# Order of the down and gate/up pieces, source of the sigmoid, and order of the bias products in a mixture-of-experts loop

## What is computed

```python
def expert_block(args):
    xb, e = args
    gu = xb @ w_gu[e] + b_gu[e]
    gate = jnp.minimum(gu[:, :D_FF], SWIGLU_LIMIT)              # limit 7.0
    up = jnp.clip(gu[:, D_FF:], -SWIGLU_LIMIT, SWIGLU_LIMIT)
    hid = (up + 1.0) * gate * jax.nn.sigmoid(SWIGLU_ALPHA * gate)
    return hid @ w_dn[e] + b_dn[e]
```

## Time and profile before

| | us |
|---|---|
| median of 3 runs | 1810.24 |
| lowest and highest | 1800.36, 1814.44 |
| profiled execution | 1814.36 |
| its span, first to last instruction | 1812.5 |

### The profile page before, as it was taken

One profiled execution on the slowest core, in us unless ns is written; L12 is line 12 of the kernel. 1 busy time (PEld: TensorE's weight loads), 2 busy tenths in 40 slices (PEclk: granted clock), 3 DMA queues, 4 the chain that ended last, 5 costly groups with the idle time before them and its releaser, 6 DMA issues.

```text
span 1812.5 us, 20603 instructions
## 1 busy us (share of the span) xinstructions
PE 1600.7 (88%) x7124; PEld 737.2 (41%) x7125; DVE 362.9 (20%) x853; ACT 372.4 (21%) x723; POOL 121.8 (7%) x219
## 2 busy tenths in 40 slices
PE   6899999999999997978779998787999886998991
PEld 4565665666666653322223332222333222332330
DVE  3443442223231123110101110101011101011114
ACT  3443342354430020111101111111111111111111
POOL 0100000000000000100001110000011000010110
PEclk9889989899999997988989999889999998999995
DMA  7112112221208524899998999999899999579894
GB/s 254 63 47 73 47 47 93 71 70 47 93 1 300 196 102 176 351 406 417 414 406 312 403 364 412 408 414 408 337 404 352 407 411 399 243 308 411 330 382 156
DMA packets 108009, 477.36 MB, mean 263 GB/s; under 512 B 12899, under 2 KB 16848, under 8 KB 74530
## 3 DMA queue, kind: packets, MB, share of 16 engines
q1 hardware_dynamic: 99928, 461.77, 64.9%
q0 software_dynamic: 7808, 15.00, 2.5%
q10 hardware_dynamic: 234, 0.08, 0.0%
HBM read 471.26 MB, written 15.50 MB: 269 GB/s over the span
## 4 chain that ended last, share of the span: by engine, by line
PE 70%; DMA 17%; DVE 6%; issue 3%; SPq 2%; ACT 1%; DVEq 0%; ACTq 0%; POOL 0%; POOLq 0%
PE bank L578 30%; PE bank L961 20%; DMA ring<-in_w_gate_up 16%; PE bank L984 15%; PE bank L582 3%; PE bank L967 1%; DVE r_c L1322 1%; DVE r_kv L1319 1%; DVE r_v L1322 1%; DMA b_router_b<-in_b_router 1%; SPq L537 0%; SPq L544 0%; SPq L453 0%; DVE r_qk L1316 0%; DVE ring L1316 0%
## 5 line engine op out<-in xcount | busy, mean ns | idle before, releaser
L961 PE MATMUL bank<-ring,r_kv 128*64 128x512 f32 x2184 | 521.1, 625 | 98.2 <-DMA ring<-in_w_gate_up 98.2
L961 PEld LDWEIGHTS bank<-ring,r_kv 128*64 128x64 f32 x2184 | 157.3, 142 | 411.6 <-issue 309.4
L984 PE MATMUL bank<-ring,r_kv 128*64 128x512 f32 x1248 | 291.4, 610 | 0.7 <-ACT r_kv L1049 0.7
L578 PE MATMUL bank<-r_xt,ring 128*128 128x336 f32 x848 | 259.7, 462 | 2.0 <-DVE r_xt L1319 1.7
L1316 DVE TENSOR_SCALAR r_kv<-bank 128x512 f32<-128x512 f32 (+1 forms) x80 | 55.0, 687 | 928.2 <-PE bank L967 921.7
L578 PEld LDWEIGHTS bank<-r_xt,ring 128*128 128x128 f32 x848 | 163.5, 196 | 85.0 <-issue 15.9
L984 PEld LDWEIGHTS bank<-ring,r_kv 128*64 128x64 f32 x1248 | 93.1, 144 | 197.6 <-issue 196.6
L1049 ACT ACTIVATE r_xt<-bank 128x512 f32<-128x512 f32 x39 | 23.3, 598 | 520.8 <-PE bank L984 520.8
L578 PE MATMUL bank<-ring 128*128 128x336 f32 (+4 forms) x336 | 94.9, 423 | 4.1 <-DVE ring L1475 3.9
L1275 ACT ACTIVATE r_o<-r_kv 128x512 f32<-128x512 f32 x39 | 24.6, 632 | 324.0 <-DVE r_kv L1316 324.0
L582 PEld LDWEIGHTS bank<-const,r_v 64*128 64x128 f32 (+3 forms) x524 | 45.5, 139 | 79.3 <-DVE r_v L1322 44.5
(11 more groups left out here) (231 smaller groups left out, 992.1 us busy)
## 6 DMA issues: line engine op xcount, KB each, us to landing
ring<-in_w_gate_up SPq DMA_DIRECT2D x256, 1024.0 KB, 18.1
ring<-in_w_down SPq DMA_DIRECT2D x128, 1024.0 KB, 15.1
ring<-in_w_in SPq DMA_DIRECT2D x12, 2048.0 KB, 7.9
ring<-in_w_proj_b SPq DMA_DIRECT2D x2, 2048.0 KB, 8.4
ring<-in_w_proj_a SPq DMA_DIRECT2D x2, 2048.0 KB, 8.5
ring<-in_w_out SPq DMA_DIRECT2D x2, 2048.0 KB, 7.9
ring<-y_rows SPq DMA_DIRECT2D x4, 1024.0 KB, 7.9
ring<-in_w_uq SPq DMA_DIRECT2D x2, 1152.0 KB, 8.9
```

The costliest lines, as they stand in the source:

```text
L578: ins = pe.matmul(out, l, r, start=(n == 0), stop=(n == len(pairs) - 1), **kw)
L961: ins = pe.matmul(half(gate_bank if q < 2 else up_bank, q % 2), xg[:, k, :], w[:, 512 * q:512 * q + 512], start=False, stop=False, skip_gr ...
L984: ins = pe.matmul(half(out_bank, t), hidT[:, j, BLK * h:BLK * h + BLK], w[:, h, 512 * t:512 * t + 512], start=(j == 0 and h == 0), stop=(j ...
```

## The change

In PE's loop `gate_up(0)` moves behind `down(1)`, and the biases are split: those of the up bank stay ahead of the transposes of `hid`, those of the gate bank come behind them. So the gate bank stays readable until `hid` is made. ACT takes the sigmoid straight from the gate bank. As the gate is no longer limited ahead of it, the limit is put on the sigmoid's result (sigmoid grows with its argument, so its minimum with sigmoid(1.702 * 7) is the same) and, for the gate itself, into the last step. DVE's steps become: `up` as the clamp of up + 1 (1 is added once to the biases of the up half, ahead of the loop), `glu` as min(sigmoid, limit) times `up`, and `hid` as min(gate bank, 7) times `glu`. The step that wrote `gt` is gone; `pick` waits for the first k-tile of its block instead.

```diff
--- before.py
+++ after.py
@@ -37,6 +37,7 @@
 SCALE = float(np.float32((NOPE + ROPE) ** -0.5))
 EPS = 1e-6
 LIMIT, ALPHA = 7.0, 1.702
+SIG_LIMIT = float(1.0 / (1.0 + np.exp(-LIMIT * ALPHA)))
 NEG = -1e30
 
 
@@ -324,7 +325,7 @@
 
         xg = r3(r_kv[:, 0:512], 8)
         hidT = r3(r_kv[:, 512:1024], 4)
-        gt = r_kv[:, 1024:1536]
+        glu = r_kv[:, 1024:1536]
         up = r_kv[:, 2048:2560]
         sg = r_o[:, 0:512]
         gateT = r_o[0:NE, 2048:2048 + NT]
@@ -376,11 +377,11 @@
              "sig_ready", "qk_ready", "tail_done", "pad_set", "ones_set", "n_set", "lg_d", "lg_a", "gates_x", "gates4",
              "wprev_ready", "e_ready", "q_scaled", "hs_v", "hs_s", "hn_ready", "q_ready", "pmax", "pnorm", "mix_a",
              "x1_ss", "x1_v", "x1_s", "x2_ready", "chosen_set", "gate_x", "gate_e", "moe_tab", "stored", "stored_c"))
-        m_glu, gates_set, kr_in = sem("m_glu"), sem("gates_set"), sem("kr_in")
+        bgu_set, gates_set, kr_in = sem("bgu_set"), sem("gates_set"), sem("kr_in")
         w_if_set = sem("w_if_set")
-        (m_xrow, m_gath, m_xg, m_gt, m_sig, m_hid, m_yrow, m_gate, m_up, m_down, m_store, m_dve, m_pick, m_turn, m_hidT,
+        (m_xrow, m_gath, m_xg, m_sig, m_hid, m_yrow, m_gate, m_up, m_down, m_store, m_dve, m_pick, m_turn, m_hidT,
          fin_v, fin_ss, fin_s, fin_out, all_out) = map(sem, (
-             "m_xrow", "m_gath", "m_xg", "m_gt", "m_sig", "m_hid", "m_yrow", "m_gate", "m_up", "m_down", "m_store",
+             "m_xrow", "m_gath", "m_xg", "m_sig", "m_hid", "m_yrow", "m_gate", "m_up", "m_down", "m_store",
              "m_dve", "m_pick", "m_turn", "m_hidT", "fin_v", "fin_ss", "fin_s", "fin_out", "all_out"))
         m_rows_in, m_read = sem("m_rows_in"), sem("m_read")
         x_sent, yrow_free = sem("x_sent"), sem("yrow_free")
@@ -944,10 +945,10 @@
             def half(bank, t):
                 return bank[BLK * t:BLK * t + BLK, :]
 
-            def bias(b):
+            def bias(b, quarters):
 
                 pe.wait_ge(m_pick, b + 1)
-                for q in range(4):
+                for q in quarters:
                     pe.matmul(half(gate_bank if q < 2 else up_bank, q % 2), pick[32 * q:32 * q + 32, :],
                               bgu[32 * q:32 * q + 32, :],
                               start=True, stop=False, skip_group_check=True)
@@ -986,8 +987,8 @@
                                         stop=(j == 3 and h == 1), skip_group_check=True)
                 ins.then_inc(m_down, 1)
 
-            pe.wait_ge(ld_bgu, 64)
-            bias(0)
+            pe.wait_ge(bgu_set, 1)
+            bias(0, (0, 1, 2, 3))
             pe.wait_ge(m_xg, 1)
             for k in range(8):
                 gate_up(k, 0)
@@ -1002,14 +1003,15 @@
                 pe.sem_inc(m_rows_in, 1)
                 tokens_turned()
                 pe.wait_ge(m_read, b + 1)
-                bias(b + 1)
+                bias(b + 1, (2, 3))
                 hidden_turned(b)
-                pe.wait_ge(m_xg, b + 2)
-                gate_up(0, e1)
+                bias(b + 1, (0, 1))
                 pe.wait_ge(m_hidT, b + 1)
                 pe.wait_ge(yrow_free, b + 1)
+                pe.wait_ge(m_xg, b + 2)
                 down(0, e)
                 down(1, e)
+                gate_up(0, e1)
                 down(2, e)
                 gate_up(1, e1)
                 down(3, e)
@@ -1271,8 +1273,8 @@
             act.wait_ge(m_gath, 1)
             signal(tokens(), m_xg, 1)
             with act.Fori(0, nb) as b:
-                act.wait_ge(m_gt, b + 1)
-                act.activation(sg, gt, ACT.Sigmoid, scale=ALPHA).then_inc(m_sig, 1)
+                act.wait_ge(m_gate, b + 1)
+                act.activation(sg, banks[2][:, :], ACT.Sigmoid, scale=ALPHA).then_inc(m_sig, 1)
                 act.wait_ge(m_gath, b + 2)
                 tokens().then_inc(m_xg, 1)
                 act.wait_ge(m_turn, b + 1)
@@ -1587,6 +1589,8 @@
                                          AX.X, ALU.add), chosen_set, t + 1)
                 signal(ts(gate[0:m, t, 0:4], top[0:m, t, 0:4], top[0:m, t, 0:1], ALU.subtract), gate_x, t + 1)
 
+            dve.wait_ge(ld_bgu, 64)
+            signal(ts(bgu[64:128, :], bgu[64:128, :], 1.0, ALU.add), bgu_set, 1)
             dve.wait_ge(ld_late, 64)
             for t in range(2):
                 out_rows(t)
@@ -1666,17 +1670,15 @@
             nb = dve.value_load(nbi[0:1, 0:1].bitcast(I32), min_val=NE, max_val=MAXB)
             dve.wait_ge(moe_tab, 1)
             with dve.Fori(0, nb) as b:
-                dve.wait_ge(m_gate, b + 1)
-                ts(gt, banks[2][:, :], LIMIT, ALU.min).then_inc(m_gt, 1)
+                dve.wait_ge(m_up, 8 * b + 1)
                 ts(pick, lane, be[:, bass.ds(dve.snap(b + 1), 1)], ALU.is_equal).then_inc(m_pick, 1)
                 dve.wait_ge(m_up, 8 * b + 8)
-                ts(up, banks[3][:, :], LIMIT, ALU.min, -LIMIT, ALU.max).then_inc(m_read, 1)
+                ts(up, banks[3][:, :], LIMIT + 1.0, ALU.min, 1.0 - LIMIT, ALU.max).then_inc(m_read, 1)
                 dve.wait_ge(m_sig, b + 1)
-                dve.wait_ge(m_gt, b + 1)
-                tt(gt, gt, sg, ALU.mult).then_inc(m_dve, 1)
                 dve.wait_ge(m_read, b + 1)
+                stt(glu, sg, SIG_LIMIT, up, ALU.min, ALU.mult).then_inc(m_dve, 1)
                 dve.wait_ge(m_dve, b + 1)
-                stt(hid, up, 1.0, gt, ALU.add, ALU.mult).then_inc(m_hid, 1)
+                stt(hid, banks[2][:, :], LIMIT, glu, ALU.min, ALU.mult).then_inc(m_hid, 1)
                 dve.wait_ge(m_hid, b + 1)
                 dve.wait_ge(m_pick, b + 2)
                 dve.wait_ge(moe_tab, 1)
```

## The result

The changed kernel took 1811.61 us (median of 22 runs, 1806.7 to 1816.1), the kernel before 1808.36 us over as many runs beside it. The ratio is 1.0021, with a 95% interval of 1.0011 to 1.0030: by it 3.8 us slower, 2.0 to 5.4. It is a small loss, and it is made of parts several times its size.

A forecast was written before the change was run, and what follows sets the result against it. Transfers were taken to bound one-block experts and PE the further blocks of an expert. Terms +9.1, +0.2, -7.7 and -1.0 sum to +0.6 us: 1811 us against a median of 1810.24, range 1803 to 1826 (the forecast's own 1804 to 1817).

The forecast's parts named there:

- nine PE-bound iterations: Iterations from each transition until DMA next starts from an empty queue: turnaround 1.01 us longer in each, +9.1 us.
- four transitions: Where the last transfer-bound iteration leads into a double expert: 25.72 us falls to 23.8 each, -7.7 us.
- start of the loop: DMA idles there waiting for the first down slot, which would be freed sooner: -1.0 us.
- last block: Block with no k-tile to run: only the longer DVE path is new there, +0.2 us.
- Bounds: Expert loop: transfers at 410 GB/s bound one-block experts; PE bounds an expert's second block, 23.6 us per iteration.
- The lost cover: Turnaround: `down(0)` must wait for ACT's copy, which `gate_up(0)` had covered; 3.56 us behind the up step, not 2.72.
- The biases: Second half of the biases, behind the transposes: about 0.6 us, fitting into the 0.69 us wait for the copy.
- DVE steps: Behind the up bank: still three steps, but `glu` now waits for the up step, +0.17 us.
- Slots at the start: First down slots freed 1.72 us sooner, less 1.01 for the turnaround, where DMA waits for them: -1.0 us.
- The late k-tile slot: After double experts `gate_up(0)` frees its slot later: costed at 0; as rival up to 18 us, chance 0.06.
- The clock rival: Longer turnaround lets PE's clock fall, 3.1 us at each of 13; chance two to five falls 0.15, six or more 0.11.

The follow-up runs named there:

- first two profiles: The changed kernel, unaltered, profiled in two executions: 1806.7 and 1817.3 us whole, loop 1071.1 and 1077.2 us.
- the order alone: Against the kernel before, only `gate_up(0)` moves behind `down(1)`; biases, sigmoid and DVE steps stay as before. Ratio 0.9986 (0.9971 to 1.0001).
- the third profile: The changed kernel, unaltered, profiled in another execution: 1810.0 us whole, loop 1071.0 us.

## Why the prediction was right, step by step

I forecast 1811 us against a median of 1810.24, in 1804 to 1817, and no change that can be told within 1%. It came out at 1811.61, and relative to before at +3.8 us instead of +0.6. That the absolute figures lie 0.6 us apart is luck: my three executions of before had a median 1.9 us above that of the 22, and the change costs 3 us more than I forecast. The mechanism is as forecast: two terms of 8 to 10 us that nearly cancel. The terms, from the first two profiles, and measured from the first refill issue:

| term | forecast, us | measured, us |
|---|---|---|
| nine PE-bound iterations | +9.1 | +10.2 (9 x 1.13) |
| four transitions | -7.7 | -8.0 |
| start of the loop | -1.0 | 0.0 |
| last block | +0.2 | 0.0 |
| sum | +0.6 | +2.2 |
| falls of the clock in PE-bound turnarounds | a rival | 0 to 4.9, mean about 2.1 |

The sum meets the loop up to the last up step, which is 2.3 us longer in the profile without a fall; with the falls' mean it gives 4.3 us, against 3.8 measured (2.0 to 5.4).

- *Bounds.* Right. The period between first gate/up pieces in transfer-bound stretches stays at 31 us, and PE's clock and idle time there moved without moving anything else.
- *The lost cover.* Right in kind. `down(0)` waits for ACT's copy, 0.84 us later than the k-tile could start; the kernel with the order alone shows exactly that.
- *The biases.* This term was too small. I took two of four quarters at about 0.6 us from 1.09 us for all four, as if they ran one behind the other. They run side by side: two take 1.07. The pair behind the transposes so sticks out by 0.17 us per iteration, and 0.84 + 0.13 + 0.17 are the 1.13 us within rounding, where I had 1.01; with the k-tile put back ahead it costs all of its 1.00.
- *DVE steps.* +0.13 us instead of +0.17. `hid` reading a bank costs nothing to be seen (0.69 us), and the up step did not start sooner.
- *Transitions.* Right: the two that the chain shows from landing to landing took 23.64 and (from 1261.93) 23.59 us, where I had 23.6 with PE warm, the third (from 1532.58) 23.89. The fourth PE no longer entered from a wait: late from the iterations ahead of it, it found its first piece landed and made the delay good. For its length I take the third profile, where the first piece landed at 1661.41, 1.5 us ahead of PE, and the next `down(0)` started at 1685.15: 23.74. PE was warm, or cold for a shorter time than before (1.94 us for the first eight matmuls in place of 3.68), and landings were the limit.
- *Slots at the start.* Wrong, if small. I counted `down(0)`'s slot as freed 1 us sooner (by my own figures, 1.72 - 1.01, it was 0.7). SP's issues, of before and of after:

```profile
707.48 12.33 SPq L540 DMA_DIRECT2D ring<-in_w_gate_up  x8
734.01 3.80 SPq L544 DMA_DIRECT2D ring<-in_w_down  x3
```

```profile
697.95 12.33 SPq L541 DMA_DIRECT2D ring<-in_w_gate_up  x8
725.14 8.95 SPq L545 DMA_DIRECT2D ring<-in_w_down  x4
```

The down refill comes 26.53 us behind the first in the one and 27.19 in the other: 0.66 us later. The first turnaround runs cold in both. The four quarters of before, and the new turnaround:

```profile
726.45 1.98 PE L951 MATMUL bank<-bgu,r_qk 32*64 32x512 f32 x8 [2.72 <-DVE r_kv L1316]
```

```profile
716.44 1.97 PE L952 MATMUL bank<-bgu,r_qk 32*64 32x512 f32 x4 [2.16 <-DVE r_kv L1318]
...
718.34 1.11 PE L583 MATMUL bank<-const,r_v 128*128 128x128 f32 x4
...
719.39 1.97 PE L952 MATMUL bank<-bgu,r_qk 32*64 32x512 f32 x4
...
721.29 5.38 PE L985 MATMUL bank<-ring,r_kv 128*64 128x512 f32 x16
```

Two pairs at 1.97 us each stand where four quarters took 1.98 together. And `down(0)` itself is now among the cold matmuls (5.38 us for 16, 3.65 warm), where before `gate_up(0)` took the cold stretch and the clock was back at 1.00 for the first slot to be freed. The loss didn't reach the loop's end: the first gate/up piece before the first transition was 232.9 us behind the start in both. The window above from 722 to 728 has a DMA share of 0.28, so the idle that I meant to shorten is still there.
- *The late k-tile slot.* No cost, as forecast: the PE-bound stretch has a DMA share of 0.89 as in the earlier trace rows, and the other terms alone give the loop's length up to the last up step (2.2 us of 2.3).
- *The clock rival.* I gave it 0.26 and took the forecast without it. It is real: none to three falls in an execution. I had its price too high (3.1 us from the last block, where the half clock lasted longer; 1.65 us in the loop), and the number from which it decides was never reached. The idle time of the turnaround is 0.23 + 0.37 us, less than my 1.3, as the bias pairs fill more; idle time alone doesn't order the kernels, since the order alone has 0.23 + 0.23 + 0.77 us and no fall.

What stays open: what in a turnaround makes the clock fall, and how many falls the kernel before has over many executions, since I have one profile of it. The 22 executions of the changed kernel had mean clocks of 0.944 to 0.951, and its four profiles 0.950 (no fall), 0.943 (three), 0.950 (none) and 0.948 (two), so they cover the same range.

## What to carry to other kernels

Before moving a piece of work into a wait, see what the piece covered where it stood, and count both in the regime in which each matters: here the wait lay in transfer-bound iterations that cost nothing, and the cover in PE-bound ones that cost everything, with the transitions between them the only gain. Then shorten the chain that the piece had covered (halves of `hid`, its transposes and its copy): order and halves gave 0.1% (not clear of noise) and 0.2% of the kernel alone and 0.9% together. Don't split a group of small matmuls that run side by side, each part costs as much as the whole.

## What the runs showed of the hardware

- Four fp32 products of 32 rows by 512 columns on four row groups took 1.09 us, two of them 1.07.
- TensorE's clock fell to 0.50 in some turnarounds that had only 0.23 and 0.37 us of idle time in them, between the pairs of biases and small transposes, and it did so in some executions of the same kernel and not in others (0, 3, 0 and 2 of 24). Taking the biases away made it fall in 12 of 24, so that a kernel with less work was slower (loop 1085.4 against 1071 to 1077 us). Moving all of them behind the transposes, with 1.77 us of idle time ahead of these, made it 13 of 24. In the kernel with all four quarters ahead of the transposes (idle 0.23, 0.23 and 0.77 us) no PE-bound iteration showed it.
- The last block of a kernel, with no k-tile in it, had the clock at 0.50 for 6.8 us before and not at all in the order alone, with the same instructions and waits: 9.98 and 7.09 us for its 32 down matmuls.
- A `hid` step that reads one operand from a bank took 0.69 us, the same as from SBUF.
